# An encoder trunk on one core: x's second half loaded behind the eighth weight chunk, biases stored in two transfers

## The reference, cut to what matters

```python
xn = rmsnorm(x, gain)
q, k, v, gate = split(xn @ w_in)           # w_in: 2048 x 8192; 8 heads, each with 2 x 128 of q and k
s = q . k + rel_bias[bucket(k_pos - q_pos)]   # the same 32 x 8 table for all positions
a = softmax(s[:, 0]) - lam * softmax(s[:, 1])
o = rmsnorm_per_head(a @ v) * head_gain * (1 - lambda_init)
x = x + (o * silu(gate)) @ w_out
# then the convolution layer: x = x + ((layer norm of conv(a * sigmoid(g))) * silu(z)) @ w_out + b
return rmsnorm(x, final_gain)
```

## Time and profile before

| | |
|---|---|
| median of 3 runs | 823.56 us (823.46 to 823.87) |
| the profiled execution | 822.98 us, its span 821.2 us |
| TensorE busy | 813.7 us (99%) |
| VectorE busy | 659.9 us (80%) |
| ScalarE busy | 460.6 us (56%) |
| GpSimd busy | 235.9 us (29%) |
| granted TensorE clock, mean | 0.998 of full speed |

### The profile page before, as it was taken

The page is one execution under the profiler, slowest core; times in us unless marked ns, Lnnn a source line. Parts: engine busy times, 40 slices in busy tenths (PEclk is TensorE's granted clock), DMA queues, the critical chain, the costliest instruction groups (busy, mean ns, idle before and its releaser), DMA issues.

```text
span 821.2 us, 13878 instructions
## 1 busy us (share of the span) xinstructions
PE 813.7 (99%) x5616; PEld 752.7 (92%) x5616; DVE 659.9 (80%) x1111; ACT 460.6 (56%) x600; POOL 235.9 (29%) x115
## 2 busy tenths in 40 slices
PE   9999999999999999999999999999999999999996
PEld 9988899889998899888888899999999999998885
DVE  7578784697658794698788987999999999569782
ACT  7756643547336543656554455455664555597562
POOL 0300010000000000002000008989889888680000
PEclk9999999999999999999999999999999999999999
DMA  9987599976654566534656557556556556556842
GB/s 329 392 298 273 186 268 352 329 186 205 216 192 153 172 195 219 191 114 156 218 191 205 191 173 233 189 191 205 184 179 204 175 188 203 183 209 226 307 152 102
DMA packets 104113, 175.21 MB, mean 213 GB/s; under 512 B 3792, under 2 KB 41168, under 8 KB 103512
## 3 DMA queue, kind: packets, MB, share of 16 engines
q1 hardware_dynamic: 99712, 163.65, 58.3%
q0 software_dynamic: 2720, 8.39, 4.5%
q10 hardware_dynamic: 1624, 2.38, 0.8%
HBM read 172.30 MB, written 12.08 MB: 225 GB/s over the span
## 4 chain that ended last, share of the span: by engine, by line
PE 99%; ACT 0%; issue 0%; POOL 0%; DVE 0%; POOLq 0%
PE ps_acc L1391 17%; PE ps_acc L1394 17%; PE ps_acc L1393 17%; PE ps_acc L1377 13%; PE ps_acc L1379 13%; PE ps_acc L1380 13%; PE ps_acc L1440 1%; PE ps_acc L1444 1%; PE ps_acc L1447 1%; PE ps_d L1497 1%; PE ps_a L1353 0%; PE ps_a L1490 0%; PE ps_d L1476 0%; PE ps_d L1478 0%; PE ps_a L1492 0%; PE ps_d L1477 0%
## 5 line engine op out<-in xcount | busy, mean ns | idle before, releaser
L535 ACT ACTIVATE sb_w_hi<-sb_w_raw 128x2048 fp32r<-128x2048 f32 x142 | 271.3, 1919 | 209.6 <-PE ps_acc L1394 142.6
L918 DVE TENSOR_TENSOR sb_w_lo<-sb_w_raw,sb_w_hi 128x2048 fp32r<-128x2048 f32 x97 | 220.3, 2289 | 80.6 <-ACT sb_w_hi L535 80.2
L490 POOL TENSOR_TENSOR sb_w_lo<-sb_w_raw,sb_w_hi 128x2048 fp32r<-128x2048 f32 x45 | 208.1, 4632 | 252.5 <-ACT sb_w_hi L535 252.5
L1391 PE MATMUL ps_acc<-sb_conv_hi,sb_w_hi 128*128 128x256 f32 x768 | 213.3, 278 | 0.0
L1394 PE MATMUL ps_acc<-sb_conv_hi,sb_w_lo 128*128 128x256 f32 x768 | 212.5, 277 | 0.0
L1393 PE MATMUL ps_acc<-sb_conv_lo,sb_w_hi 128*128 128x256 f32 x768 | 212.4, 277 | 0.0
L1149 DVE SCALAR_TENSOR_TENSOR ps_d<-sb_uT,sb_dwT,ps_d 128x256 f32<-128x256 f32 x480 | 188.9, 480 | 4.5 <-ACT ps_d L770 4.5
L1377 PE MATMUL ps_acc<-sb_w_hi,sb_act_hi 128*128 128x512 f32 x384 | 149.9, 390 | 0.0
L1379 PE MATMUL ps_acc<-sb_w_lo,sb_act_hi 128*128 128x512 f32 x384 | 149.7, 390 | 0.0
L1380 PE MATMUL ps_acc<-sb_w_hi,sb_act_lo 128*128 128x512 f32 x384 | 149.5, 389 | 0.0
L1393 PEld LDWEIGHTS ps_acc<-sb_conv_lo,sb_w_hi 128*128 128x128 f32 x768 | 144.3, 188 | 0.0
(11 more groups left out here) (209 smaller groups left out, 892.2 us busy)
## 6 DMA issues: line engine op xcount, KB each, us to landing
sb_w_raw<-in_attn_w_in SPq DMA_DIRECT2D x59, 1024.0 KB, 7.3
sb_w_raw<-in_conv_w_in SPq DMA_DIRECT2D x64, 512.0 KB, 4.6
sb_w_raw<-in_attn_w_out SPq DMA_DIRECT2D x16, 1024.0 KB, 5.1
sb_w_raw<-in_conv_w_in SPq DMA_DIRECT2D x16, 1024.0 KB, 5.1
sb_w_raw<-in_conv_w_out SPq DMA_DIRECT2D x15, 1024.0 KB, 5.0
weight_sums<-in_conv_w_out POOLq DMA_DIRECT2D x6, 1024.0 KB, 12.1
sb_w_raw<-weight_sums SPq DMA_DIRECT2D x4, 1024.0 KB, 5.8
sb_w_raw<-in_attn_w_in SPq DMA_DIRECT2D x15, 256.0 KB, 4.5
```

Of the source, the lines that this page charges most:

```text
L490: pool.tensor_tensor(w_part(w_lo, c), w_raw[c % RING][:], w_part(w_hi, c).bitcast(F32), ALU.subtract).then_inc(lo_ready_pool, 1)
L535: act.activation(w_part(w_hi, c if like is None else like), w_raw[slot][:], ACT.Copy).then_inc(hi_ready, 1)
L918: dve.tensor_tensor(w_part(w_lo, like), w_raw[slot][:], w_part(w_hi, like).bitcast(F32), ALU.subtract).then_inc(lo_ready, 1)
L1391: pe.matmul(into, left_hi, hi[:, kt], start=(kt == 0 and f % 2 == 0), stop=False, skip_group_check=True)
```

## The change

It does four things, in the first pair of heads but for one wait in the later pairs.

1. SyncE loads the second half of x's rows behind chunk 7 instead of behind chunk 6.
2. ScalarE makes the high part of chunk 7 ahead of the second half's squares, and VectorE its low part ahead of 1/rms. Both stood behind q's parts before.
3. The store of the windows is cut in two: heads 0 and 1 where the whole store stood, heads 2 to 7 in slot 8, after a wait for the first store.
4. SyncE loads the first pair's bias behind chunk 11 instead of behind chunk 13, waiting for the first store; the bias of the later pairs waits for both stores.

```diff
--- before.py
+++ after.py
@@ -401,15 +401,16 @@
                             sp.dma_start(w_raw[0][:, HALVES[1]], w_in[:, HALVES[1], D:D + GW]).then_inc(landed[0], 16)
                             continue
                         load(i, w_in[:, i * CK:(i + 1) * CK, bass.ds(t * D + j * GW, GW)])
-                        if first and t == 1 and i in (1, 2):
-                            st = i - 1
+                        if first and t == 1 and i in (1, 3):
+                            st = i // 2
                             sp.dma_start(xs[:, st], x_rows[:, st]).then_inc(rows_landed[st], 16)
                         if first and t == 1 and i == NCH - 1:
                             sp.dma_start(dwT[:], taps).then_inc(taps_landed, 16)
-                        if (t, i) == ((3, 1) if first else (0, NCH - 1)):
+                        if (t, i) == ((2, NCH - 1) if first else (0, NCH - 1)):
                             if first:
                                 sp.wait_ge(windows_stored, 16)
                             else:
+                                sp.wait_ge(windows_stored, 32)
                                 sp.wait_ge(max_ready, 4 * j)
                             sp.dma_start(bias_w[:], windows_dram[bass.ds(j * 2, 2)].rearrange("h p i -> p h i")
                                          ).then_inc(bias_landed, 16)
@@ -582,7 +583,8 @@
                                accum_out=ss[:, st:st + 1]).then_inc(ss_ready, 1)
                 act.wait_ge(ss_ready, st + 1)
                 if st == 0:
-                    high_part(RING + 2, 2, 2)
+                    for i in (2, 3):
+                        high_part(RING + i, i, 2)
             act.wait_ge(ms_ready, 1)
             act.activation(sd, ms, ACT.Sqrt).then_inc(sd_ready, 1)
             def empty_acc(G, par, dst, func, scale):
@@ -598,6 +600,15 @@
                 for f in range(2):
                     act.activation(q_parts[0][:, 2 * f:2 * f + 2].rearrange("p a s -> p (a s)"), acc[:, f], ACT.Copy
                                    ).then_inc(q_hi_ready, 1)
+
+            def store_windows(first, upto):
+
+                act.wait_ge(line_stored, 16)
+                if first:
+                    act.wait_ge(windows_stored, 16)
+                act.dma_start(windows_dram[first:upto], bass.AP(line_dram.tensor, line_dram.offset + P - 1 + first * REL,
+                                                                [[REL, upto - first], [-1, P], [1, BW]])
+                              ).then_inc(windows_stored, 16)
 
             def pair_slot(j, i):
 
@@ -616,9 +627,9 @@
                     high_of_q(j)
                 if i == 4 and type(j) is int and j == 0:
 
-                    act.wait_ge(line_stored, 16)
-                    act.dma_start(windows_dram, bass.AP(line_dram.tensor, line_dram.offset + P - 1,
-                                                       [[REL, HEADS], [-1, P], [1, BW]])).then_inc(windows_stored, 16)
+                    store_windows(0, 2)
+                if i == 8 and type(j) is int and j == 0:
+                    store_windows(2, HEADS)
                 if i == 8:
                     for f in range(2):
                         act.wait_ge(k_ready, 2 * j + f + 1)
@@ -659,7 +670,6 @@
                                    ).then_inc(split_hi, 1)
 
             high_of_q(0)
-            high_part(RING + 3, 3, 2)
             for i in range(NCH, 16):
                 if i == 7:
                     act.wait_ge(a_full, 2)
@@ -960,7 +970,7 @@
                 dve.tensor_tensor(w_part(w_lo, RING)[:, HALVES[half]], w_raw[0][:, HALVES[half]],
                                   w_part(w_hi, RING)[:, HALVES[half]].bitcast(F32), ALU.subtract
                                   ).then_inc((half_lo, lo_ready)[half], 1)
-            for i in range(1, NCH - 1):
+            for i in range(1, NCH):
                 low_part(RING + i, i)
             dve.wait_ge(ss_ready, 2)
             norm_factor(1, 1)
@@ -1053,7 +1063,7 @@
                             dve.scalar_tensor_tensor(
                                 cols, cols, o_rstd[:, 2 * st + h:2 * st + h + 1], g_rows[:, st, h * VD:(h + 1) * VD],
                                 ALU.mult, ALU.mult).then_inc(m_ready, 1)
-                if not by_pool(16 * j + i + RING):
+                if (type(j) is not int or (j, i) != (0, 3)) and not by_pool(16 * j + i + RING):
                     low_part(16 * j + i + RING, i % NCH, pair_chunk(j, i + RING))
                 if i == 15:
```

## The result

The changed kernel takes 830.03 us (median of 6 runs, 829.58 to 830.89), the kernel before 823.71 (6 runs). The ratio is 1.0074, 95% interval 1.0061 to 1.0087. The forecast was 823.1 with a range up to 824.2. Rival (a), slower because the first store is late, is what happened, though larger than the 824 to 827 at which it was priced for the likely T. The profiled execution took 829.58 us with a span of 827.8, against 822.98 and 821.2: 6.6 us to find.

What follows compares the result with a forecast made beforehand. TensorE, busy 813.7 of 821.2 us, was taken to bound the kernel. Removing its waits of 0.21 us at chunk 7 and 0.28 us before the product with v would bring 823.56 to 823.1 us, range 822.4 to 824.2.

Steps and rivals of the forecast that it cites:

- Rival (a): First store late, so chunk 12 and the attention weights are late for TensorE: 824 to 827 us mostly; chance 9%.
- What bounds the kernel, and the most that can be won: TensorE bounds; its waits at chunk 7 and before the product with v allow at most 0.49 us.
- Part 1: Loading x's second half behind chunk 7 removes TensorE's wait there; 1/rms comes 2.73 us later, within 1.89 us left, costing nothing.
- its 0.21 us: TensorE's wait at chunk 7, after the 1/rms transposes, for VectorE's low part; forecast to go.
- Part 2, the store's end T: The two-head window store, issued at 41.4, would end at 50.5 us, between bounds of 43.7 and 63.1.
- 68 a us of the middle row: Packet rate from the old store's traffic (205 in 3 us), giving the two-head store 3.8 us once moving.
- The bound of 63.1: Latest end of the two-head store, taking 21.7 us as for all eight heads; total then 833.3 us.
- The rule that I weighed, turns between queues: DMA engines alternate between queues packet by packet; by it the two-head store would be over before 47 us.
- The price behind T: Chunk 12 lands 6.1 us after the first store's end, its low part at 10.25 us, then VectorE's first score tile.
- One us of lateness costs TensorE one: Once VectorE begins the first score tile later than before, at 63.42, each us costs TensorE one.
- 53.2: First-store end, in us, above which VectorE is later than before at the first score tile (63.42 less 10.25).
- The hold on ScalarE: ScalarE's wait for the first store, ahead of k's high parts; not held up with that end near 50.5.

Runs made afterwards that it cites:

- The winning version: Changed kernel with the line kept 16 times in HBM, each head of the first store its own transfer with outermost dimension 16; 822.51 us, ratio 0.9981.
- order only: Kernel before with only x's second half and the parts of chunk 7 moved, one store of all eight heads; 824.25 us, ratio 1.0006.
- store only: Changed kernel with x's second half and the parts of chunk 7 put back in their old order; 829.30 us, ratio 1.0067.
- second store later: Changed kernel with the six-head store and ScalarE's wait in slot 12 instead of 8; 826.35 us, ratio 1.0038.
- outer dimension 4: Changed kernel with the line kept 16 times in HBM, each head of the first store its own transfer with outermost dimension 4; 828.94 us, ratio 1.0062.
- four heads first: Changed kernel with four heads in the first store and four in the second; 831.46 us in one run.
- bias late: Changed kernel with the first pair's bias load back behind chunk 13; 827.64 us, ratio 1.0048.

## Why the prediction was wrong

- **What bounds the kernel, and the most that can be won: right.** The winning version has no wait left where the two were, and its rows are 0.51 us shorter from the transposes to the product. The rest of its lead is not explained by rows.
- **Part 1: right.** Chunk 7's low part began at 37.49 (37.0), the reciprocal at 41.88 (38.85, so 3.03 later, not 2.73), chunk 7 followed the transposes in 0.13 us. No wait for 1/rms in any kernel with the moved order. Not foreseen: alone, part 1 delays the whole store and with it the bias, and gives its 0.21 us back.
- **Part 2, the store's end T: this step failed.** T was 55.73, not 50.5. The issue came 0.9 us earlier than said (40.47 against 41.4), and the first packets moved after 44.5, about the forecast 4 us later; what was wrong is the rate. The prediction took the rate of the store of before, "68 a us of the middle row" and 41 at worst, for a property of the queue, and divided fewer packets by it. That rate belonged to eight engines, one for each head of the outermost dimension. With two heads the engines fall with the bytes: 256 packets at 33 a us are 7.8 us at best, and beside the loads it was slower still (25 packets in 46 to 48 us). The bound of 63.1, "if the size did not matter", was nearest to the mechanism and was given too little. The rule that I weighed, turns between queues, was not the one that decides here. "DMA: Bandwidth & Descriptors" of the Trainium skill has that one (Why a DMA increments its semaphore by 16 and not by 1): the number of engines of a transfer is the largest up to 16 that divides the slowest dimension of both patterns. By that rule the trace agrees: 13.4% busy for two heads, 26.6% for four, 49.2% for eight, which is 2.1, 4.3 and 7.9 of 16 engines.
- **The price behind T: right without competition; with it this step failed too.** T + 10.25 was measured as T + 9.97 where the six-head store was out of the way, and T + 14.3 in the changed kernel. I had let that store share the engines "as the one store did before", at no cost, though the row for 6.1 us came from a moment when no store ran.
- **One us of lateness costs TensorE one: right.** The first tile was 6.59 us later than before, the product with v 6.56. The same pair is 0.65 and 0.63 in "order only", 5.87 and 5.85 in "store only", 1.86 and 1.83 in "second store later", 4.82 and 4.80 with outer dimension 4, 8.46 and 8.44 with four heads first, whether TensorE stopped at the scores or not. The 6.56 are the two terms above: 55.73 - 53.2 = 2.53 for T, and 14.28 - 10.25 = 4.03 for the price behind it. At the price of rival (a), T - 53.2 - 0.21, the 55.73 would have been 2.3 us. The 0.21 does not come off: what is won at chunk 7 becomes a longer wait at the product with v.
- **The stop at the score banks: not foreseen.** VectorE's lateness reached TensorE there first, stopped it for 3.4 us and left it at half speed for a while. In the changed kernel both lie inside VectorE's lateness and add nothing to it; in "bias late", where TensorE came last, they set the time.
- **The hold on ScalarE: seen, not priced.** "Held up" was judged by T near 50.5. At 60.69, in "bias late", it stopped TensorE for 3.09 us.

## What to carry to other kernels

Before a transfer is cut in pieces, look at how many DMA engines each piece will run on: the busy share of a queue while it is alone tells it (0.13 is two of sixteen). Cutting along the outermost dimension makes pieces with fewer engines, and a quarter of the bytes may take as long as the whole (here 20.4 us for either, beside the loads). Where a wait for such a piece goes in front of other work of a queue, price what is queued behind it at the piece's worst end, not its likely one.

## What the runs showed of the hardware

- HBM to HBM rows of 1.5 KB moved at 15 to 16.5 packets a us for each engine: 33 a us for two heads and 65 for four, with nothing or next to nothing beside them, and 121 for eight, with as many packets of loads beside them.
- Beside a full stream of loads it was about 7 a us for each engine, for eight heads as for two: in 50 to 54 us 231 packets of the store of before, and 54 packets of the two-head store in "bias late".
- ScalarE's queue issued the first store at 40.47, while the table load that stands ahead of the root ran on the engine until 41.63 and q's high parts, also ahead of the store in program order, began at 41.75. So the sentence above on the bias, that a DMA issue waits in its engine's queue like any other instruction, is not borne out here: the issue did not wait for these instructions to run.
